# Lagged expert order, release-ordered weight units and three-pass output projections in a two-layer decoder kernel

## The chip, the cores and the metric

The kernel runs on one core of one Trainium2 chip. The metric is the device time of one execution in microseconds (us); lower is better. Engines are named as in the profile: PE is TensorE's matmul stream, PEld its loads of stationary operands, DVE is VectorE, ACT is ScalarE, POOL is GpSimd and SP is SyncE, which here only issues DMAs, in order.

## What is computed

A decoder trunk of two layers on 512 tokens of width 1024, in float32:

```python
for i in range(DEPTH):                      # DEPTH = 2
    if i % 2 == 0:                          # even: RWKV-7 heads beside sparse attention
        y = concatenate([rwkv7_time_mix(h), dsa_sparse_attention(h)])
        x = x + y @ ev_w_out                # 1024 x 1024
    else:                                   # odd: stick-breaking attention
        x = x + stick_breaking_attention(h) @ od_w_out
    x = x + hierarchical_moe(rmsnorm(x))    # top-1 of 4 groups, top-2 of 8 experts in it
return rmsnorm(x)
# an expert: (silu(xb @ w1) * (xb @ w3)) @ w2 ; w1, w3: 1024 x 512, w2: 512 x 1024 ; 32 experts a layer
```

All 32 experts' weights are read in each layer: 32 x 6 MB.

## The kernel before

A layer is a row of stages with a barrier between them: the mixer's stages (`even_mixer` or `odd_mixer`), `router`, `experts`. Tokens come in four tiles of 128.

**Weight units.** `ExpertWeights` (line 603) holds eleven units of 2 MB in SBUF. A piece is one matrix of one expert, numbered 3n + part (w1, w3, w2 of expert n), and piece p goes to unit p mod 11 (`place`, line 593). Units 8 and 9 (`GUEST`) hold the output projection's two halves until it is done; units 0 to 7 come free with the end of the mixer. SP loads pieces 0 to 7 at the start of `router` (line 358), piece 8 when all eight groups of the output projection are done, then waits for the scatter of the sorted rows, loads rows for three experts, and loads piece 9; piece 10 is the first of `experts` (line 863). From there `freed` (line 865) waits, piece by piece, for the unit's former user: `up_done` for w1 and w3, `down_done` for w2. The last two experts' w1 and w3 come in halves of 1 MB (`HALVED`). After the last piece SP loads, into units 8 and 9, what the next stage needs: three 1 MB chunks of the odd layer's projection in the first layer (`LoadedAhead`), the final gain in the second.

**Router.** For each tile i, PE does the output projection in two groups of 512 columns (h = 0, 1), each eight products of 128x128 by 128x512 in float32 (`out_project`, line 371). DVE adds each group to x (`add`, line 467); then PE transposes the tile (`turn`), DVE and ACT copy the transposed tile over the tile's place in `yT` (`empty_turned`, line 472, and line 445), and PE takes the router's logits from it (`logits`). PE's order is written out by hand: group (i+1, 0), turn(i), two of the eight steps of (i+1, 1), logits(i), the other six. DVE's first work in the stage is the scaling of the router's weights (line 513), which waits for their DMAs.

**Experts.** For each expert n, `up_expert` multiplies 48 rows by w1 and w3 (the two run beside each other in two column halves of the array, lines 723 and 724), `turn_hidden` transposes the hidden rows, `down_expert` multiplies by w2 (line 753), and `spread` (line 775) takes the result to the tokens by a selection matrix, in three-pass form; DVE adds it to x (line 820). `turn_rows` (line 711) transposes the next expert's rows. For n below `OWN` = 19 PE is lagged: up(n) is followed by turn_hidden(n-1) and down(n-1), with spread(n-2) in between. From `OWN` on each expert's up is followed by its own down, with spread(n-1). Between the two orders PE does down(18) before up(19) (lines 912 to 914).

**Three passes.** `three_passes` (line 1292) splits float32 operands into a rounded high part (fp32r, made by ACT) and a rest (fp32r, made by DVE) and multiplies high by high, high by low and low by high. The projections into q, k, v use it already.

**Chunks and attention of the even layer.** `rwkv_chunks` (line 2262) works on each tile by repeated squaring of small matrices, `squares(lv)` and `update(lv)`; `gram` (line 2395) makes products into two banks that DVE must have emptied. DVE fills gaps with `search.rounds` of the top-k search. `sparse_attend` (line 2669) goes through 16 units (4 tiles x 4 pairs of heads; 4 units for each length of 512, 384, 256, 128 keys): PE makes scores of two heads, DVE adds the mask (line 2752), DVE takes the negated maximum (line 2755), ACT takes the exponential and its sum (line 2792), DVE scales (line 2765), PE transposes, ACT copies, PE multiplies by the values.

## Time and profile before

| | |
|---|---|
| device time, three runs | 1745.83, 1750.96 (median), 1755.37 us |
| the profiled execution | 1747.62 us, span 1745.9 us |
| PE busy | 1632.2 us, 93% of the span |
| DVE, ACT, POOL busy | 56%, 26%, 9% |
| DMA moved | 475.40 MB, mean 272 GB/s |

PE is the clock of the whole kernel by its busy share, but the share is an average: in the two expert stages (about 478 to 950 us and 1261 to 1735 us) the DMA engines are also full. A row of the timeline gives the start, the duration, the engine, the line, the operation, the tiles and the count, then idle time in front in square brackets with its releaser. A float32 product is two PE instructions in the profile.

### The profile page before, as it was taken

The page shows a single profiled execution, that of the slowest core. Times are in us where ns is not written, and L with a number is a line of the kernel's source. Part 1 is how long each engine was busy: PE and PEld are TensorE (multiplying, and loading weights), DVE is VectorE, ACT ScalarE, POOL GpSimd, SP SyncE. Part 2 cuts the span into 40 slices and gives each one's busy share as a digit, 9 for nine tenths or more (in the row PEclk, how much of TensorE's full clock was granted, in tenths as well). Part 3 has the DMA queues.
Part 4 walks back from the last instruction along what each step waited for, and adds up shares of the span by engine and source line. Part 5 has one row for each costly group of instructions (what it writes and reads, how often), then busy time and mean ns, then how long its engine had stood idle before and what let it go on. Part 6 is the DMA issues. An engine that isn't in the chain of part 4 may idle for free. (4 is left out here: it accounts for less than half of the span.)

```text
span 1745.9 us, 27516 instructions
## 1 busy us (share of the span) xinstructions
PE 1632.2 (93%) x11158; PEld 875.4 (50%) x11287; DVE 977.9 (56%) x1657; ACT 459.5 (26%) x777; POOL 157.0 (9%) x188
## 2 busy tenths in 40 slices
PE   7999877889899999999998999999899999999996
PEld 6756666655533333333334977665533333333333
DVE  4548566581336666676666322561336666666666
ACT  4353444372311111111112321462211111111112
POOL 2002524310100000000000040120100000000000
PEclk9999999999999999999999999999999999999998
DMA  6441000028599999999996250208699999999993
GB/s 200 115 127 55 7 3 4 5 96 307 230 370 425 426 425 425 427 425 424 426 422 229 77 193 24 97 2 332 227 384 425 427 424 425 426 426 425 425 421 160
DMA packets 102256, 475.40 MB, mean 272 GB/s; under 512 B 28913, under 2 KB 67825, under 8 KB 76528
## 3 DMA queue, kind: packets, MB, share of 16 engines
q1 hardware_dynamic: 98752, 461.03, 65.5%
q0 software_dynamic: 3376, 12.58, 1.9%
q8 instruction: 91, 1.49, 0.4%
q14 instruction: 37, 0.30, 0.0%
HBM read 454.71 MB, written 18.87 MB: 271 GB/s over the span
## 5 line engine op out<-in xcount | busy, mean ns | idle before, releaser
L723 PE MATMUL ps<-w_unit,xT 128*48 128x512 f32 x1024 | 451.9, 594 | 3.8 <-DVE xT L780 3.0
L724 PE MATMUL ps<-w_unit,xT 128*48 128x512 f32 x1024 | 452.0, 594 | 0.0
L820 DVE SCALAR_TENSOR_TENSOR x<-ps,gate_by_expert,x 128x512 f32<-128x512 f32 x512 | 348.3, 744 | 178.2 <-PE ps L775 178.1
L723 PEld LDWEIGHTS ps<-w_unit,xT 128*48 128x48 f32 x1024 | 125.9, 123 | 308.9 <-issue 305.5
L753 PE MATMUL ps<-w_unit,hidT 128*48 128x512 f32 x1024 | 247.2, 603 | 12.1 <-issue 12.1
L775 PE MATMUL ps<-y_high_low,slots_to_tokens 128*128 128x512 f32 x512 | 154.3, 422 | 8.1 <-DVE y_high_low L795 5.2
L843 ACT ACTIVATE y_high_low<-ps 48x512 fp32r<-48x512 f32 x128 | 75.8, 592 | 322.1 <-PE ps L753 320.5
L775 PEld LDWEIGHTS ps<-y_high_low,slots_to_tokens 128*128 128x128 f32 x512 | 86.1, 188 | 123.2 <-DVE x L820 57.0
L1294 PE MATMUL ps<-hT_high,w_high 128*128 128x512 f32 (+1 forms) x336 | 135.5, 403 | 7.1 <-PE ps L1296 4.0
L836 ACT ACTIVATE gate_act_hid<-ps 48x512 f32<-48x512 f32 x64 | 37.9, 593 | 372.3 <-PE ps L724 372.3
L1296 PE MATMUL ps<-hT_high,w_low 128*128 128x512 f32 (+1 forms) x336 | 133.0, 396 | 0.0
L1295 PE MATMUL ps<-hT_low,w_high 128*128 128x512 f32 (+1 forms) x336 | 132.5, 394 | 0.0
L724 PEld LDWEIGHTS ps<-w_unit,xT 128*48 128x48 f32 x1024 | 125.9, 123 | 0.0
L753 PEld LDWEIGHTS ps<-w_unit,hidT 128*48 128x48 f32 x1024 | 60.0, 122 | 119.2 <-issue 119.2
L788 DVE TENSOR_TENSOR gate_act_hid<-gate_act_hid,ps 48x512 f32<-48x512 f32 x64 | 44.3, 692 | 127.9 <-ACT gate_act_hid L836 110.9
L377 PE MATMUL ps<-w_unit,yT 128*128 128x512 f32 x256 | 113.8, 596 | 1.7 <-PEq L78 1.7
L795 DVE TENSOR_TENSOR y_high_low<-ps,y_high_low 48x512 fp32r<-48x512 f32 x128 | 88.1, 688 | 25.7 <-ACT y_high_low L843 22.7
L1294 PEld LDWEIGHTS ps<-hT_high,w_high 128*128 128x128 f32 (+1 forms) x336 | 63.3, 188 | 33.1 <-issue 17.7
L377 PEld LDWEIGHTS ps<-w_unit,yT 128*128 128x128 f32 x256 | 47.3, 190 | 54.6 <-issue 54.6
L1296 PEld LDWEIGHTS ps<-hT_high,w_low 128*128 128x128 f32 (+1 forms) x336 | 63.2, 188 | 15.1
L1295 PEld LDWEIGHTS ps<-hT_low,w_high 128*128 128x128 f32 (+1 forms) x336 | 63.3, 188 | 14.5 <-issue 0.2
L1278 DVE TENSOR_TENSOR w_low<-w_unit,w_high 128x2048 fp32r<-128x2048 f32 (+1 forms) x13 | 28.6, 2196 | 60.3 <-ACT w_high L1264 60.2
(368 smaller groups left out, 1972.2 us busy)
## 6 DMA issues: line engine op xcount, KB each, us to landing
w_unit<-in_moe_w SPq DMA_DIRECT2D x184, 2048.0 KB, 28.3
w_unit<-in_moe_w SPq DMA_DIRECT2D x16, 1024.0 KB, 33.0
x_rows<-sorted_rows SPq DMA_DIRECT2D x64, 192.0 KB, 26.5
w_unit<-in_od_w_qkv SPq DMA_DIRECT2D x12, 1024.0 KB, 5.5
w_raw<-in_ev_w_in SPq DMA_DIRECT2D x10, 1024.0 KB, 6.1
sorted_rows<-bias SPq DMA_DIRECT2D x32, 192.0 KB, 5.6
w_unit<-in_ev_w_out SPq DMA_DIRECT2D x2, 2048.0 KB, 10.6
w_unit<-in_od_w_out SPq DMA_DIRECT2D x2, 2048.0 KB, 11.3
```

The lines of the kernel that those rows point to most:

```text
L377: last = nc.tensor.matmul(ps_out[2 * (i % 2) + h][:, :], yT[:, f, tok(i)], w[h][:, f, :], start=f == 0, stop=f == KD - 1)
L723: nc.tensor.matmul(ps_1[0:MB, :], xT[b][:, k, :], w1[:, k, :], start=k == 0, stop=k == KD - 1)
L724: last = nc.tensor.matmul(ps_3[UP:UP + MB, :], xT[b][:, k, :], w3[:, k, :], start=k == 0, stop=k == KD - 1)
L753: last = nc.tensor.matmul(ps_y[h][half[h], :], hidT[:, k, :], w2[:, k, h * FF:(h + 1) * FF], start=k == 0, stop=k == KF - 1)
L775: nc.tensor.matmul(ps_c[t % 2 * 2 + h][:, :], sel_of(n)[:, t * P:(t + 1) * P], y[:, h, :], start=True, stop=True).then_inc(spread_out, 1)
L788: nc.vector.tensor_tensor(hid, gate_act, ps_3[UP:UP + MB, :], ALU.mult).then_inc(hid_done, 1)
L795: nc.vector.tensor_tensor(y[half[1 - h], h, :], ps_y[h][half[h], :], y[half[h], h, :].bitcast(F32), ALU.subtract).then_inc(low_out, 1)
L820: nc.vector.scalar_tensor_tensor(out=xs, in0=ps_c[i % 4][:, :], scalar=gate(t), in1=xs, op0=ALU.mult, op1=ALU.add).then_inc(added, 1)
L843: nc.scalar.activation(y[half[h], h, :], ps_y[h][half[h], :], ACT.Copy).then_inc(high_out, 1)
L1294: nc.tensor.matmul(out, lhsT[0], rhs[0], start=start, stop=False)
L1295: nc.tensor.matmul(out, lhsT[0], rhs[1], start=False, stop=False)
L1296: return nc.tensor.matmul(out, lhsT[1], rhs[0], start=False, stop=stop)
```

## The change

- `OWN` becomes 31 from 19: all experts but the last are lagged.
- Units are given to pieces in the order in which the lagged order releases them (`in_order_of_release`, `places`), and `freed` waits accordingly.
- The first four pieces behind the eleven (3's w2 and 4's w1, w3, w2) come in halves of 1 MB, each issued when its unit's first or second half has been used (`load_early`).
- Expert 0 uses another PSUM bank, and the transposes of expert 1's rows move into the middle of up(0).
- Tiles 1 to 3 of the output projections go in three passes. Their high parts live in units 5, 6 and 7 (`LENT`), their low parts over the originals (`wl` is units 8 and 9, `yT_low` lies over `yT`). ACT makes the high parts: 8 weight pieces of 1024 columns and 3 tiles. DVE makes the low parts.
- So only pieces 0 to 4 are loaded at the start of `router`. Pieces 5 and 8 are issued at the seventh group, pieces 6, 7 and 9 behind the scatter and the rows.
- What is loaded ahead for the next stage waits for each guest unit's own last user.
- In `rwkv_chunks` the gram product of the second kind goes behind update(1), and two search rounds go in front of its reading on DVE.
- In `sparse_attend` the add and the maximum become one `tensor_tensor_reduce` for each head, and scores are kept negated.

```diff
--- before.py
+++ after.py
...
+    y_high, y_low, w_high, w_low = (c.sem(n) for n in ("y_high", "y_low", "w_out_high", "w_out_low"))
+    w_out, lent = wts.guest(), wts.lent()
+    wh, yT_high, wl = lent[0:2], lent[2], lent[3:5]
...
-            wts.load(sp, range(GUEST[0]))
-            sp.wait_ge(out_done, 2 * TT)
+            wts.load(sp, range(LENT[0]))
+            sp.wait_ge(out_done, 2 * TT - 1)
+            wts.load(sp, LENT[:1])
             wts.load(sp, GUEST[:1])
             for j in range(2):
                 sp.wait_ge(scattered[j], 16 * TT)
             for n in range(SLOTS):
                 r.load_rows(sp, xrows, n, n * CAP)
+            sp.wait_ge(out_done, 2 * TT)
+            wts.load(sp, LENT[1:])
             wts.load(sp, GUEST[1:])
...
-                    last = nc.tensor.matmul(ps_out[2 * (i % 2) + h][:, :], yT[:, f, tok(i)], w[h][:, f, :],
-                                            start=f == 0, stop=f == KD - 1)
+                    out = ps_out[2 * (i % 2) + h][:, :]
+                    if i == 0:
+                        last = nc.tensor.matmul(out, yT[:, f, tok(i)], w[h][:, f, :], start=f == 0, stop=f == KD - 1)
+                    else:
+                        if f == 0:
+                            pe.wait_ge(y_low, i)
+                        if i == 1 and f % 2 == 0:
+                            pe.wait_ge(w_low, h * HALF + f // 2 + 1)
+                        last = three_passes(nc, out, [part[:, f, tok(i)] for part in (yT_high, yT_low)],
+                                            [part[h][:, f, :] for part in (wh, wl)], f == 0, f == KD - 1)
...
+            def round_tile(i):
+                nc.scalar.activation(yT_high[:, :, tok(i)], yT[:, :, tok(i)], ACT.Copy).then_inc(y_high, 1)
+
+            round_tile(1)
+            for h in range(2):
+                act.wait_ge(wts.guest_in[h], 16)
+                for f in range(0, KD, 2):
+                    nc.scalar.activation(wh[h][:, f:f + 2, :], w_out[h][:, f:f + 2, :], ACT.Copy).then_inc(w_high, 1)
+                round_tile(2 + h)
...
+            def lower_tile(i):
+                dve.wait_ge(y_high, i)
+                V.tensor_tensor(yT_low[:, :, tok(i)], yT[:, :, tok(i)], yT_high[:, :, tok(i)].bitcast(F32),
+                                ALU.subtract).then_inc(y_low, 1)
+
+            def lower_weights(h, n):
+                dve.wait_ge(out_done, h + 1)
+                dve.wait_ge(w_high, h * HALF + n + 1)
+                fs = slice(2 * n, 2 * n + 2)
+                V.tensor_tensor(wl[h][:, fs, :], w_out[h][:, fs, :], wh[h][:, fs, :].bitcast(F32),
+                                ALU.subtract).then_inc(w_low, 1)
+
+            lower_tile(1)
+            lower_tile(2)
+            for n in range(HALF):
+                lower_weights(0, n)
             add(0, 0)
             add(0, 1)
+            lower_weights(1, 0)
+            lower_weights(1, 1)
             for i in range(LAST):
+                if i == 0:
+                    lower_weights(1, 2)
+                    lower_weights(1, 3)
+                    lower_tile(3)
                 add(i + 1, 0)
...
+LENT = (5, 6, 7)
...
+LAST, OWN = N_EXP - 1, N_EXP - 1
+
+
+def in_order_of_release():
+
+    pieces = [(0, 0), (0, 1)]
+    for n in range(1, OWN):
+        pieces += [(n, 0), (n, 1), (n - 1, 2)]
+    pieces += [(OWN - 1, 2)]
+    for n in range(OWN, N_EXP):
+        pieces += [(n, 0), (n, 1), (n, 2)]
+    return pieces
+
+
+def places():
+
+    released, where, uses = in_order_of_release(), {}, [0] * UNITS
+    for p in range(N_EXP * len(PARTS)):
+        j = p if p < UNITS else where[released[p - UNITS]][0]
+        where[divmod(p, len(PARTS))] = j, uses[j]
+        uses[j] += 1
+    return released, where, uses
+
+
+RELEASED, PLACES, LOADS = places()
...
+EARLY = [divmod(p, len(PARTS)) for p in range(UNITS, UNITS + 4)]
+IN_HALVES = EARLY + [(n, part) for n in HALVED for part in range(2)]
...
-    ps_x, ps_h, ps_y, ps_1, ps_3, ps_c = ps[0], ps[1], (ps[2], ps[2]), ps[3], ps[3], ps[4:8]
+    ps_x, ps_h, ps_y, ps_c = ps[0], ps[1], (ps[2], ps[2]), ps[4:8]
+    ps_up = lambda n: ps[4] if isinstance(n, int) and n == 0 else ps[3]
...
-    LAST, OWN = N_EXP - 1, 19
...
-        if not isinstance(n, int) or n >= 1:
+        if not isinstance(n, int) or n >= 2:
...
+            if isinstance(n, int) and n < len(EARLY) // 2 and k == KD // 2 - 1:
+                last.then_inc(up_half, 1)
...
+            if n == 0:
+                turn_rows(pe, 1, 0)
...
+        if isinstance(n, int) and n == 1:
+            act.wait_ge(hid_done, n)
...
+            def load_early(gone):
+                for half_, done in enumerate((up_half, up_done)):
+                    sp.wait_ge(done, gone + 1)
+                    for piece in EARLY[2 * gone:2 * gone + 2]:
+                        wts.load_half(sp, *piece, half_)
 
             for n in range(SLOTS, N_EXP):
                 sp.wait_ge(xT_done, n - SLOTS + 1)
                 r.load_rows(sp, xrows, slot(n), n * CAP)
-                if n in HALVED:
+                if n - SLOTS < 2:
+                    load_early(n - SLOTS)
+                elif n in HALVED:
...
-                sp.wait_ge(down_done, max(users) + 1)
-                ahead.load(sp, [wts.unit[j] for j in GUEST])
+                ahead.load(sp, [wts.unit[j] for j in GUEST], lambda i: sp.wait_ge(down_done, users[i] + 1))
...
             up_expert(pe, 0, -1)
-            turn_rows(pe, 1, 0)
...
                     squares(lv)
-                    if lv == 1:
-                        gram((B[2], B[3]), ka, both, False, 2 * CH)
                     if lv > 1:
                         update(lv - 1)
+                    if lv == 2:
+                        gram((B[2], B[3]), ka, both, False, 2 * CH)
...
+                before, between, behind, last = ROUNDS[t]
+                search.rounds(dve, min(2, before))
                 for par in range(2):
                     o = B[2 + par].read(dve)[:, :].rearrange("p (f m n) -> p f m n", f=FT, m=2)
                     B[2 + par].empty(V_.tensor_tensor(NQ[:, par, :, :, :], o, later, ALU.mult))
-                before, between, behind, last = ROUNDS[t]
-                search.rounds(dve, before)
+                search.rounds(dve, before - min(2, before))
...
-                        pe.wait_ge(biased, i - 1)
+                        pe.wait_ge(maxed, 2 * i - 2)
...
-                    bias = m.bias[:, t, 0:L].rearrange("p (o l) -> p o l", o=1).to_broadcast([P, 2, L])
-                    V_.tensor_tensor(lg[i % DEEP][:, :, 0:L], ps_z[i % 2][:, :, 0:L], bias,
-                                     ALU.add).then_inc(biased, 1)
-                    dve.wait_ge(biased, i + 1)
-                    V_.tensor_reduce(nmax[:, i, :], lg[i % DEEP][:, :, 0:L], AX.X, ALU.max,
-                                     negate=True).then_inc(maxed, 1)
+                    for a in range(2):
+                        V_.tensor_tensor_reduce(out=lg[i % DEEP][:, a, 0:L], in0=ps_z[i % 2][:, a, 0:L],
+                                                in1=m.bias[:, t, 0:L], scale=-1.0, scalar=-4.0 * NEG, op0=ALU.add,
+                                                op1=ALU.min, accum_out=nmax[:, i, a:a + 1]).then_inc(maxed, 1)
...
+                        act.wait_ge(maxed, 2 * i + a + 1)
                         nc.scalar.activation(lg[i % DEEP][:, a, 0:L], lg[i % DEEP][:, a, 0:L], ACT.Exp,
-                                             bias=nmax[:, i, a:a + 1], accum_out=tot[:, i, a:a + 1]).then_inc(exped, 1)
+                                             bias=nmax[:, i, a:a + 1], scale=-1.0, accum_out=tot[:, i, a:a + 1]).then_inc(exped, 1)
...
```

`up(1)` waits for no other expert's product any more, since expert 0 has its own bank; the view functions, `arrived` and the semaphores of the halves are changed to match.

## Rows read from the trace of the kernel before

**Rows 1.** The page: what the DMA engines moved in each fortieth of the span.
```profile
GB/s 200 115 127 55 7 3 4 5 96 307 230 370 425 426 425 425 427 425 424 426 422 229 77 193 24 97 2 332 227 384 425 427 424 425 426 426 425 425 421 160
```
**Rows 2.** Three stretches; last columns: TensorE clock, DMA share, GB/s.
```profile
490.00:500.00 10.00, 8.50 (x42) 3.00 (x41) 1.25 (x2) 0.59 (x1) 0.00 (x0) 1.00 0.93 366
500.00:510.00 10.00, 9.96 (x50) 3.91 (x50) 3.64 (x6) 2.11 (x4) 0.00 (x0) 1.00 0.69 273
...
1285.00:1290.00 5.00, 5.00 (x26) 1.76 (x24) 2.52 (x5) 1.18 (x2) 0.00 (x0) 1.00 0.42 128
```
**Rows 3.** PE's timeline: two row transposes; up(29), up(31) of either layer.
```profile
682.32 0.55 PE L711 MATMUL ps<-ident,x_rows 128*128 128x128 f32 x3
696.31 0.55 PE L711 MATMUL ps<-ident,x_rows 128*128 128x128 f32 x3
...
899.25 0.60 PE L723 MATMUL ps<-w_unit,xT 128*48 128x512 f32 x1 [0.78 <-DMA w_unit<-in_moe_w]
...
928.31 0.59 PE L723 MATMUL ps<-w_unit,xT 128*48 128x512 f32 x1
...
1681.66 0.59 PE L723 MATMUL ps<-w_unit,xT 128*48 128x512 f32 x1
...
1710.69 0.59 PE L723 MATMUL ps<-w_unit,xT 128*48 128x512 f32 x1
```
**Rows 4.** PE's timeline where the lagged order ends, layer one then two.
```profile
743.70 0.68 PE L745 MATMUL ps<-ident,gate_act_hid 48*128 48x48 f32 x4
...
751.38 1.92 PE L753 MATMUL ps<-w_unit,hidT 128*48 128x512 f32 x8
...
1525.76 0.68 PE L745 MATMUL ps<-ident,gate_act_hid 48*128 48x48 f32 x4
...
1530.14 3.26 PE L753 MATMUL ps<-w_unit,hidT 128*48 128x512 f32 x8
...
1536.49 0.59 PE L723 MATMUL ps<-w_unit,xT 128*48 128x512 f32 x1
```
**Rows 5.** SP's timeline: the first rows' loads in layer one and two.
```profile
478.45 1.28 SPq L1052 DMA_DIRECT2D x_rows<-sorted_rows  x3
...
1260.78 1.28 SPq L1052 DMA_DIRECT2D x_rows<-sorted_rows  x3
```
**Rows 6.** PE's timeline: output projection in either layer; first and last of 14 passes.
```profile
398.12 20.84 PE L377 MATMUL ps<-w_unit,yT 128*128 128x512 f32 x48 [0.92 <-PEq L78]
...
1180.54 20.84 PE L377 MATMUL ps<-w_unit,yT 128*128 128x512 f32 x48 [0.76 <-PEq L78]
...
1029.82 0.39 PE L1294 MATMUL ps<-hT_high,w_high 128*128 128x512 f32 x1
...
1032.84 0.39 PE L1295 MATMUL ps<-hT_low,w_high 128*128 128x512 f32 x1
```
**Rows 7.** DVE and ACT in the router's stage, and DVE's split of weights.
```profile
405.10 0.49 DVE L513 TENSOR_TENSOR w_router<-w_router,moe_gain 128x320 f32<-128x320 f32 x1 [10.92 <-DMA w_router<-in_moe_router_expert]
...
1189.45 0.49 DVE L513 TENSOR_TENSOR w_router<-w_router,moe_gain 128x320 f32<-128x320 f32 x1 [12.59 <-DMA w_router<-in_moe_router_expert]
...
952.90 1.23 DVE L1278 TENSOR_TENSOR w_low<-w_unit,w_high 128x1024 fp32r<-128x1024 f32 x1
...
412.85 1.06 ACT L442 ACTIVATE xn<-x 128x1024 f32<-128x1024 f32 x1 [16.45 <-DVE x L470]
```
**Rows 8.** Sparse attention by form; the page's row of line 820.
```profile
L2752 DVE TENSOR_TENSOR prob<-ps,bias 128x1024 f32<-128x1024 f32 x4 | 4.9, 1220 | 1.4 <-PE ps L2707 1.4
L2755 DVE TENSOR_REDUCE minus_max<-prob 128x2 f32<-128x1024 f32 x4 | 4.9, 1220 | 0.1
...
L2792 ACT ACTIVATION_READ_ACCUMULATOR prob<-prob,minus_max 128x1 f32 x32 | 6.0, 189 | 0.0
...
L820 DVE SCALAR_TENSOR_TENSOR x<-ps,gate_by_expert,x 128x512 f32<-128x512 f32 x512 | 348.3, 744 | 178.2 <-PE ps L775 178.1
```
**Rows 9.** Chunks of the even layer: PE at its gram product (four such waits).
```profile
286.93 1.10 PE L2402 MATMUL ps<-kk_r,k 64*64 64x128 f32 x32 [1.76 <-DVE QbT L2628]
```

More of the change, by code:

```diff
@@ L589, with rounded_over @@
 GUEST = (8, 9)
+LENT = (5, 6, 7)
 EXTRA = (0, 1, 2)
+LAST, OWN = N_EXP - 1, N_EXP - 1
[15 more added lines that the diff above has]
+RELEASED, PLACES, LOADS = places()
 def place(n, part):
-    use, j = divmod(len(PARTS) * n + part, UNITS)
-    return j, use
+    return PLACES[n, part]
 HALVED = (N_EXP - 2, N_EXP - 1)
-LOADS = [sum(place(n, part)[0] == j for n in range(N_EXP) for part in range(len(PARTS))) for j in range(UNITS)]
+EARLY = [divmod(p, len(PARTS)) for p in range(UNITS, UNITS + 4)]
+IN_HALVES = EARLY + [(n, part) for n in HALVED for part in range(2)]
+def rounded_over(c, name, shape, side):
+    with ExitStack() as once:
+        return c.sb(name, shape, F32R, ctx=once, side=side)
 class ExpertWeights:
@@ L638, in load_half @@
         eng.dma_start(self.view(n, part)[:, rows, :], expert(self.dram[part], n, 2 * k)[:, rows, :]).then_inc(
-            self.rest_landed[HALVED.index(n)][part] if half else self.landed[place(n, part)[0]], 16)
+            self.rest_landed[n, part] if half else self.landed[place(n, part)[0]], 16)
     def arrived(self, pe, n, part):
@@ L1537, in odd_mixer @@
     ctx = c.ctx.enter_context(ExitStack())
+    yT_low = rounded_over(c, "yT_low", [P, KD, T], "left")
     yT = c.sb("yT", [P, KD, T], ctx=ctx)
```

48 lines of the change are left out of this document (29 added, 19 removed).

## The prediction

> **What bounds the kernel now.** I read the slices of the DMA engines first. In both expert stages they move 422 to 427 GB/s in every slice but those at their ends [rows 1]; I take 425. An expert needs three pieces of 2048 KB and 192 KB of rows, 6.49 MB; at 425 GB/s that is 15.27 us. PE takes less: the lagged order has a period of 13.99 us, and two experts of the order without lag take 29.06, so 14.53 each [rows 3]. DMA is thus slower than PE by 1.28 us an expert, and what hides it is the lead of the eleven units. The lead is used up at the end: up(29) waits 0.78 us for its weights [rows 3]. So at up(29) of layer one both limits meet, and in layer two they nearly do. From there on the stage's end is set by what PE still has to do, two periods without lag up to up(31). What a faster PE saves before up(29) it will lose in waits; what counts is when the weights of expert 29 land, and the PE work behind it.
>
> **When the weights land.** DMA is continuous from the load of the rows (478.45 and 1260.78 [rows 5]) but for small holes. Holes from 490 to 510: 0.7 + 3.1 = 3.8 us; in layer two 0.58 x 5 = 2.9 us [rows 2]. They come from waits for units to be freed. A piece is 2.097 MB, 4.93 us. When the rows are issued, nine pieces are there now; after the change seven (0 to 5 and 8), since 6, 7 and 9 are issued behind the scatter. That costs 2 x 4.93 = 9.86 us of DMA per layer. The early halves close the holes: behind the rows the queue has pieces 6, 7, 9 and 10, 20 us of work, and up(0) frees half a unit before that. So the holes' 3.8 and 2.9 are gained in full; at worst none.
>
> **The router's length.** In float32 48 instructions, 24 products, take 20.84 us, 0.868 a product; 13 steps of one pass take 3.02 us, so three passes 0.697 [rows 6]. 48 products (tiles 1 to 3) at 0.171 save 8.2 us. By the Trainium skill (FP8 and Floating Point Precision, TensorE Precision Notes) true float32 is four passes; three would be 0.651 and save 10.4, and the sum would be some 4 us lower over both layers. The row has three passes at four fifths, and it decides.
>
> Against that stand the splits. ACT has 8 weight pieces and 3 tiles of 1024 columns at 1.06 each [rows 7], 11.7 us, inside tile 0's 13.9 us of float32 products. DVE is the tight one. It begins behind the scaled router weights, 405.6, 7.5 us after PE's first product, and 9.4 us after it in layer two [rows 6, 7]. Then, at 1.23 a split [rows 7] (about 1.2 apart): two tiles and four weight pieces, two adds of 0.69, four more pieces, tile 3, an add and the copy of tile 0's transposes. From 405.6 this is 11 x 1.2 + 3 x 0.65 + 0.65 = 15.8, so 421.4. PE, unheld, has done tile 1's first half at 412.0 + 5.6, turn(0) 0.9 and two steps 1.4: 419.9, and then the logits need that copy. PE stands 1.5 us in layer one and, DVE being 1.9 later, 3.4 in layer two. Net the router is shorter by 6.7 and 4.8. Bounds: 8.2 if DVE's splits are covered, 0 if they are half as long again. A stand at the logits holds nothing else up: positions and destinations come a tile later.
>
> So expert 29's weights land, in layer one, at 899.25 - 6.7 - 3.8 + 9.9 = 898.6. In layer two, where nothing shows the landing, I take the same distance from the rows' issue as in layer one, 420.8, less 0.9 for the smaller holes: 1680.7; up(29) began at 1681.66 [rows 3], which fits. It becomes 1680.7 - 4.8 - 2.9 + 9.9 = 1682.9. PE by itself could be there over 20 us earlier (shorter router, ten periods at 13.99 for 14.53, and the end of the lag, 9.5, not yet paid), so DMA sets this point.
>
> **The work behind it.** Lagged, up(29) is followed by two periods, 28.0 us. Then the lag ends: turn_hidden(30), a wait for DVE to split what down(29) has just left, spread(29), down(30), up(31). At 19 this took 743.70 to 753.2 (the last down at 751.38 and 1.85 of it), 9.5 us, and 1525.76 to 1536.49, 10.7 us, in layer two, where the down behind the wait ran 3.26 us in place of 1.92, as at a lower clock [rows 4]. So up(31) starts at 898.6 + 28.0 + 9.5 = 936.1 against 928.31, and at 1682.9 + 28.0 + 10.7 = 1721.6 against 1710.69 [rows 3]: **+7.8 and +10.9 us**. Before, the end of the lag was paid at expert 19, in front of DMA's limit, where the lead covered it; now it comes behind. Weights of 30 and 31 don't bind: 31's second halves are 30.5 us behind 29's, up(31) 37.5. From up(31) the order is the old one. The third chunk loaded ahead now waits for down(31), some 14 us after up(31), but is wanted third in the next stage; two are issued at down(29). I count nothing; if the next stage stood for it, 2 us.
>
> **The even layer's two stages.** In sparse attention DVE's add and maximum take 1.22 each for 512 keys and two heads [rows 8], 2.44 a unit. The fused form is two instructions; the nearest row in kind, one that combines a PSUM and an SBUF operand twice, takes 0.744 for 512 [rows 8]. With nothing for the accumulator it is 1.49; with ACT's accumulator read, 0.189 [rows 8], each, 1.87. So 0.6 to 0.95 saved a unit at 512 keys, and less at fewer, where fixed costs double: over 16 units 2.5 to 7.5 us of some 46, the lower end nearer since two short ops replace one. At half rate it would lose 2. I take -4. The Trainium skill (VectorE: DVE Perf Modes, Two Vector instructions with no wait between them) says an op that also writes its accumulator is two instructions, an argument against the fused form; ACT has such reads, 32 of them [rows 8], and no row of DVE shows one.
>
> In the chunks PE stands 1.76 us in front of the second gram product for DVE [rows 9], in each of four tiles. Moved behind update(1) it lets the squares go on, but then 1 us of gram lies in front of squares(3), which had been waiting for ACT anyhow, and DVE reads later. At most 7 us, at least 0 (DVE's two rounds could be late for the next user of the bank): I take -4.
>
> **The sum.** Against the profiled execution's 1747.62: +7.8 + 10.9 - 4 - 4 = +10.7, so **1758.3 us**. The runs' median, 1750.96, lies 3.3 above that execution, and the three runs spread over 9.5; that spread is why 0.5% (8.8 us) is about what can be told from no change here.
>
> **Rivals.**
> *The expert stages are PE's* (faster). If DMA had a reserve when PE asks sooner, so that an expert's 6.49 MB came within 13.99 us (464 GB/s; the point of decision), every saving of PE would stay: per layer the router's 6.7 or 4.8 and 12 x 0.54 = 6.5 of lag. That is -13.2, -11.3 and -8 for the even stages: 1715. For it: PE is busy 93% and shows one wait for weights in 64 experts. Against it: 425 GB/s in slice after slice, the same to 1%, however PE's period was at the time. 0.10.
> *The gains at their upper ends* (same). Attention 7, chunks 6, and the splits are covered: -5 and -5 more, 1749. For it: DVE is nearly full in attention. 0.23.
> *The three passes save nothing.* If DVE's splits or ACT's strided pieces take half as long again, PE stands the 6.7 and 4.8 that it was to save, and the weights start later by as much: 1758.3 + 11.5 = 1770. For it: layer two has a margin of less than nothing already. 0.12.
> *My forecast*, 1751 to 1765: 0.55; six parts in ten of it lie above 0.5%.
>
> **Chances.** Faster by over 0.5%: 0.10 and 0.03 of the second rival, 0.13. Slower: 0.33 and 0.12, 0.45. Within: 0.42. The range leaves out the first rival and half of the third: 1744 to 1770; forecast and second rival make it so wide.
>
> **What would show it.** PE waiting about 1.3 us for weights at most experts from about the thirteenth, up(29) near 899 and 1683 less 8 for the stages in front, and 37 to 39 us from it to up(31). DMA slices at 425. An issue of rows 5 to 7 us sooner after the router's start. PE standing 1 to 4 us before tile 0's logits. Wrong would be: no waits for weights, or up(29) more than 5 us sooner; a fused op of over 0.95 us at 512 keys; output projection steps above 0.75.

## The result and the profile after

The changed kernel takes 1772.49 us (median of four runs, 1768.29 to 1775.84) against 1753.16 (1745.83 to 1786.35) for the kernel before on the same chip: ratio 1.0138, interval 1.0116 to 1.016; the ratio is taken over fast executions alone, which leaves out 1786.35 (the other three have a median of 1750.96, which alone gives 1.0123). It is slower, by more than I forecast: 1758.3 us, range 1744 to 1770. That is 21 to 24 us where I had forecast 10.7. The profiled execution is the longest of its four, 1775.84 us; that is 28.2 above the profiled execution of before, of which about 6 seem to be that execution's own and not the change's, as the parts below show.

The page of the kernel after. Its weights' line, 811, was line 723 before:

```profile
GB/s 197 113 124 54 7 3 4 59 42 262 285 423 424 426 426 425 426 424 426 425 419 91 96 184 6 96 4 262 267 422 425 425 425 426 426 425 425 426 419 74
...
L811 PE MATMUL ps<-w_unit,xT 128*48 128x512 f32 x1024 | 454.1, 596 | 35.6 <-DMA w_unit<-in_moe_w 35.6
```

DMA moves 422 to 426 GB/s in the full slices of the stages (419 in the last of them), as in [rows 1]. New is the last column of line 811: PE idles 35.6 us ahead of its up products for weights, where the timeline of before shows a single wait of 0.78 us in both expert stages [rows 3].

PE's timeline after, the same instructions as in [rows 3]: up(15) and up(16), up(29) and up(31) of layer one, then of layer two.

```profile
682.81 0.60 PE L811 MATMUL ps<-w_unit,xT 128*48 128x512 f32 x1 [0.84 <-DMA w_unit<-in_moe_w]
698.06 0.60 PE L811 MATMUL ps<-w_unit,xT 128*48 128x512 f32 x1 [1.05 <-DMA w_unit<-in_moe_w]
...
898.74 0.60 PE L811 MATMUL ps<-w_unit,xT 128*48 128x512 f32 x1 [0.98 <-DMA w_unit<-in_moe_w]
...
938.84 0.59 PE L811 MATMUL ps<-w_unit,xT 128*48 128x512 f32 x1
...
1700.03 0.60 PE L811 MATMUL ps<-w_unit,xT 128*48 128x512 f32 x1 [0.98 <-DMA w_unit<-in_moe_w]
...
1738.90 0.59 PE L811 MATMUL ps<-w_unit,xT 128*48 128x512 f32 x1
```

698.06 - 682.81 = 15.25: from up(15), the first that waits, every expert takes DMA's time and not PE's 13.99 us. Most periods up to up(29) are 15.2, a few 15.6 to 16.2, and the mean is 15.42. Before, up(31) came 29.06 us behind up(29); now it comes 40.10 and 38.87 behind it. Between these two nothing waits for weights. What lies there is the end of the lag, at expert 31 in place of 19 (compare [rows 4]). PE's timeline after, in layer one:

```profile
926.96 0.68 PE L837 MATMUL ps<-ident,gate_act_hid 48*128 48x48 f32 x4
930.24 2.04 PE L867 MATMUL ps<-y_high_low,slots_to_tokens 128*128 128x512 f32 x4 [2.61 <-DVE y_high_low L887]
932.22 3.66 PE L845 MATMUL ps<-w_unit,hidT 128*48 128x512 f32 x8
...
937.08 1.92 PE L845 MATMUL ps<-w_unit,hidT 128*48 128x512 f32 x8
```

DVE's low part of expert 29 holds PE 2.61 us, and the down product behind it takes 3.66 us for 1.92: stretches after have PE's granted clock at 0.50 there (columns as in [rows 2]):

```profile
932.00:936.00 4.00, 4.00 (x10) 0.86 (x10) 1.92 (x3) 0.00 (x0) 0.00 (x0) 0.50 0.95 304
```

**The books.** SP issues the first rows at 473.51 and 1273.58:

```profile
473.51 1.29 SPq L1152 DMA_DIRECT2D x_rows<-sorted_rows  x3
...
1273.58 1.28 SPq L1152 DMA_DIRECT2D x_rows<-sorted_rows  x3
```

PE's first product of the output projection is at 394.37 (398.12 in [rows 6]). I take as a router stage's start SP's first issue in it, 0.05 us earlier in layer one of either kernel, 1180.49 and 1192.73 in layer two.

| stretch | before | after | predicted change | measured change |
|---|---|---|---|---|
| start to router 1 | 398.06 | 394.32 | -8 | -3.7 |
| router 1 to rows | 80.39 | 79.19 | -6.7 | -1.2 |
| rows to up(29) | 420.80 | 425.23 | +6.1 | +4.4 |
| up(29) to up(31) | 29.06 | 40.10 | +8.4 | +11.0 |
| up(31) to router 2 | 252.18 | 253.89 | 0 | +1.7 |
| router 2 to rows | 80.29 | 80.85 | -4.8 | +0.6 |
| rows to up(29) | 420.88 | 426.45 | +6.0 | +5.6 |
| up(29) to up(31) | 29.03 | 38.87 | +9.7 | +9.8 |

The two lines of the router are what I had wrong: 10.9 us of savings that did not come. The first line is partly this execution's own (eleven of the twelve runs below have the even layer's new stages, and their first router stage starts between 386.0 and 393.1, in the middle at 390.3), and so is the fifth (252.2 or 253.9 in one run or another, with either kernel's loads ahead). Against the forecast these two lines make 6.0 us. From the first masked scores of the sparse attention (350.10 and 349.44) to the router's start it is 47.96 us before and 44.88 after; the other 0.7 us of the first line's 3.7 come from the stages ahead of attention, where b_even, below, gains 4.5 and a_whole 8.9. So it is there that this execution was slow; no other execution of the kernel after has a trace.

**The router.** The three passes do what they should. PE's timeline in tile 1's first group and at tile 0's logits, then DVE's splits up to there:

```profile
410.96 0.40 PE L1397 MATMUL ps<-w_rounded,w_rounded 128*128 128x512 f32 x1
...
411.66 0.40 PE L1397 MATMUL ps<-w_rounded,w_rounded 128*128 128x512 f32 x1
...
416.66 1.95 PE L411 MATMUL ps<-w_router,yT 128*128 128x40 f32 x16 [0.46 <-DVE yT L498]
```

```profile
401.55 2.35 DVE L539 TENSOR_TENSOR yT_low<-yT,w_rounded 128x1024 fp32r<-128x1024 f32 x2
403.82 4.62 DVE L546 TENSOR_TENSOR w_rounded<-w_unit,w_rounded 128x1024 fp32r<-128x1024 f32 x4
...
414.10 1.22 DVE L539 TENSOR_TENSOR yT_low<-yT,w_rounded 128x1024 fp32r<-128x1024 f32 x1
```

411.66 - 410.96 = 0.70 a product, as worked out, and the eleven splits hold PE 0.46 us at tile 0's logits (0.70 in layer two), where I had 1.5 and 3.4. What takes the saving away stands some 40 us later, where I had not looked. ACT's and PE's timelines after, at tile 3:

```profile
459.55 1.06 ACT L465 ACTIVATE xn<-x 128x1024 f32<-128x1024 f32 x1 [12.02 <-DMA sorted_rows<-xn,dest]
...
460.61 0.58 ACT L468 ACTIVATE yT<-ps 128x512 f32<-128x512 f32 x1
```

```profile
454.07 1.06 PE L411 MATMUL ps<-w_router,yT 128*128 128x40 f32 x8 [0.43 <-DVE yT L498]
461.24 1.93 PE L411 MATMUL ps<-w_router,yT 128*128 128x40 f32 x8 [6.11 <-ACT yT L468]
```

For the normalization ACT squares each tile and throws the squares into `xn[i % 2]`, the buffer from which the scatter of tile i-2 reads. Tile 3's squares therefore wait for tile 1's scatter, and ACT's half of the copy of the transposed tile 3, which PE's last logits need, stands behind the squares in ACT's queue. ACT waits 12.02 us, PE 6.11 (13.51 and 7.59 in layer two). Before there was such a wait too, a tile earlier, and it cost nothing. ACT's and PE's timelines before:

```profile
449.44 1.06 ACT L442 ACTIVATE xn<-x 128x1024 f32<-128x1024 f32 x1 [9.55 <-DMA sorted_rows<-xn,dest]
...
463.18 1.06 ACT L442 ACTIVATE xn<-x 128x1024 f32<-128x1024 f32 x1 [6.22 <-DVE x L470]
```

```profile
464.79 1.95 PE L397 MATMUL ps<-w_router,yT 128*128 128x40 f32 x16 [0.43 <-DVE yT L475]
```

Behind the stand PE's clock is lower, though a_late, below, shows that this is not the stand's doing alone. Stretches after (columns as in [rows 2]):

```profile
445.00:455.00 10.00, 9.37 (x60) 8.16 (x58) 3.89 (x17) 2.30 (x2) 3.03 (x4) 1.00 0.95 389
455.00:460.00 5.00, 0.12 (x2) 0.01 (x1) 0.00 (x0) 0.45 (x1) 0.81 (x1) 0.83 0.97 359
460.00:465.00 5.00, 3.76 (x24) 3.76 (x25) 1.72 (x11) 4.75 (x6) 0.00 (x0) 0.50 0.19 76
...
490.00:500.00 10.00, 9.96 (x49) 3.68 (x49) 2.26 (x4) 1.07 (x3) 0.00 (x0) 1.00 1.00 424
500.00:510.00 10.00, 10.00 (x49) 4.26 (x49) 4.20 (x7) 1.96 (x4) 0.00 (x0) 1.00 1.01 416
```

After PE stood from 455 to 460 its granted clock is 0.50 from 460 to 465, the lower of its two levels. From 445 to 460 the DMA engines are full: SP issues units 5 and 8, 4.2 MB, at the seventh group (443.5 to 444.3), and POOL issues tile 1's scatter at 445.35, right behind. The last rows show the holes of [rows 2] closed, as predicted.

### The profile page after: what moved, and what is told of

It is laid out like the page before. It is cut to its first block and busy times, and to the rows that moved or that the text cites. A ratio compares the mean times of both kernels' runs of the same rounds, so it can differ in the third digit from the quotient of the medians.

```text
span 1774.0 us, 27826 instructions
## 1 busy us (share of the span) xinstructions
PE 1635.0 (92%) x11254; PEld 911.5 (51%) x11383; DVE 990.1 (56%) x1711; ACT 480.6 (27%) x799; POOL 155.5 (9%) x188
## 5 line engine op out<-in xcount | busy, mean ns | idle before, releaser
L811 PE MATMUL ps<-w_unit,xT 128*48 128x512 f32 x1024 | 454.1, 596 | 35.6 <-DMA w_unit<-in_moe_w 35.6
L811 PEld LDWEIGHTS ps<-w_unit,xT 128*48 128x48 f32 x1024 | 123.9, 124 | 338.5 <-issue 338.3
L812 PEld LDWEIGHTS ps<-w_unit,xT 128*48 128x48 f32 x1024 | 123.9, 124 | 0.0
L112 PE MATMUL ps<-half 128*128 128x128 bf16 x772 | 57.6, 236 | 7.0 <-PEq L78 6.8
L1634 DVE TENSOR_TENSOR_SCAN tail<-keep,zero 128x512 f32<-128x512 f32 (+3 forms) x64 | 49.4, 814 | 23.1 <-POOL keep L1621 23.1
L880 DVE TENSOR_TENSOR gate_act_hid<-gate_act_hid,ps 48x512 f32<-48x512 f32 x64 | 44.2, 691 | 30.0 <-ACT gate_act_hid L930 15.6
## 6 DMA issues: line engine op xcount, KB each, us to landing
w_unit<-in_ev_w_out SPq DMA_DIRECT2D x2, 2048.0 KB, 10.7
```

The costliest lines, as they stand in the source:

```text
L112: nc.tensor.matmul(ps[:, 0:P], c.half[:, :], c.half[:, :], start=True, stop=True)
L811: nc.tensor.matmul(ps_up(n)[0:MB, :], xT[b][:, k, :], w1[:, k, :], start=k == 0, stop=k == KD - 1)
L812: last = nc.tensor.matmul(ps_up(n)[UP:UP + MB, :], xT[b][:, k, :], w3[:, k, :], start=k == 0, stop=k == KD - 1)
L1634: nc.vector.tensor_tensor_scan(tail[i % DEEP][:, a, 0:L][:, ::-1], keep[i % DEEP][:, a, 0:L][:, ::-1], zero[:, 0:L], 1.0, ALU.mult, ALU.ad ...
```

## The experiments

Two theories. **A**: in each expert stage the end of the lag, about 10 us of PE's time, was hidden at expert 19 because PE led there, and is paid in full behind the point that DMA sets. **D**: the scatter that ACT's squares wait for stands behind the loads of the lent units, and this costs the router what three passes save. Rivals of A: the weights' order and the later loads cost it; rival of D: DVE's splits, or the scatter by itself. In the table d is the distance from the rows' issue to up(29), layer one / layer two; before has 420.8 / 420.9. The last three columns are from one profiled execution of each. The runs were made on several chips, each beside the kernel before on the same chip (medians 1745.9 to 1748.6 us), so runs are compared by their ratios.

| run | median us | ratio [interval] | router to rows | d | up(29) to up(31) |
|---|---|---|---|---|---|
| a_own19 | 1753.78 | 1.0035 [1.0016, 1.0053] | 79.3 / 80.4 | 427.2 / 427.9 | 29.1 / 29.0 |
| b_own31 | 1764.42 | 1.0089 [1.0066, 1.0113] | 80.5 / 80.3 | 420.0 / 419.6 | 38.9 / 40.3 |
| a_late | 1760.46 | 1.0068 [1.0047, 1.0090] | 72.6 / 73.7 | 425.5 / 426.1 | 38.9 / 39.0 |
| a_no3p | 1751.51 | 1.0019 [1.0003, 1.0035] | 81.2 / 80.3 | 416.5 / 415.6 | 39.4 / 39.0 |
| a_hold | 1773.47 | 1.0153 [1.0133, 1.0174] | 70.8 / 73.0 | 435.6 / 436.0 | 38.7 / 37.6 |
| b_even | 1739.92 | 0.9960 [0.9945, 0.9976] | 80.5 / 79.8 | 421.3 / 419.0 | 29.0 / 29.0 |
| a_no3p_own19 | 1737.19 | 0.9937 [0.9922, 0.9951] | 80.6 / 80.1 | 419.4 / 419.5 | 29.0 / 29.0 |
| a_own19_late | 1739.44 | 0.9959 [0.9944, 0.9973] | 72.5 / 73.6 | 426.3 / 426.8 | 29.0 / 29.0 |
| a_no3p_own25 | 1743.70 | 0.9974 [0.9960, 0.9988] | 80.2 / 80.2 | 423.5 / 423.5 | 29.0 / 29.0 |
| a_own25 | 1761.55 | 1.0077 [1.0061, 1.0094] | 79.3 / 80.0 | 433.8 / 433.7 | 29.0 / 29.0 |
| a_whole | 1770.44 | 1.0127 [1.0111, 1.0143] | 79.1 / 80.3 | 426.0 / 425.9 | 39.0 / 38.9 |
| a_own13_late | 1736.18 | 0.9934 [0.9911, 0.9956] | 72.5 / 73.9 | 425.2 / 426.4 | 29.1 / 29.0 |

**The end of the lag, undone and done alone.** In the kernel after, back to 19:

```diff
-LAST, OWN = N_EXP - 1, N_EXP - 1
+LAST, OWN = N_EXP - 1, 19
```

> The changed kernel with OWN back at 19, so that the lag ends at expert 19 again; units still go by the order of release. Theory A (the end of the lag costs when it lies behind the point where DMA sets the pace): up(29) stays where it is in either layer, up(31) comes 29 us behind it instead of 38.9 to 40.1, so about 20 us are saved over both layers and the kernel stands 2 to 8 us above the one before. Rival B (the slower time comes from the router and the later loads alone, the place of the lag's end is indifferent): no change to within 5 us of the changed kernel's +24. Rival C (the lag hides PE work that shows again without it): up(29) comes later by up to 6 us a layer and the saving is under 10 us in all.

It gave back 1.38% - 0.35% = about 1.0%, 18 us. In the kernel before, `OWN` from 19 to 31 and nothing else:

```diff
-    LAST, OWN = N_EXP - 1, 19
+    LAST, OWN = N_EXP - 1, N_EXP - 1
```

> The kernel before with OWN = 31 and nothing else, units in their old order. Theory A: up(29) still lands with DMA, at its old distance of 420 to 421 us from the rows' issue, PE waits for weights at most experts from the thirteenth or so, up(31) is 38 to 39 us behind up(29), and the kernel is 19 to 22 us slower than before. Rival B: within 5 us of the kernel before, since PE saves 6.5 us a layer and pays the end once as ever.

It lost 0.9%, 16 us. The point up(29) moves by at most 2.0 us against the rows in either run, while the piece behind it changes by 9.8 to 11.3: theory A, from both sides. I had expected 19 to 22 us of b_own31; its profiled execution, the longest of its four, is 21 above that of before, its median 16. The waits begin at up(19), not at the thirteenth. In b_own31 PE's timeline of layer one has up(29) where it was, waiting for weights a little longer than in [rows 3], and only then turn_hidden(30), with which the lag's end begins:

```profile
898.77 0.60 PE L723 MATMUL ps<-w_unit,xT 128*48 128x512 f32 x1 [0.97 <-DMA w_unit<-in_moe_w]
...
926.99 0.68 PE L745 MATMUL ps<-ident,gate_act_hid 48*128 48x48 f32 x4
```

**The squares freed of the scatter.** The squares go into a scratch tile, and ACT waits for the scatter only ahead of the scaled rows, which do need `xn`:

```diff
-                if i >= 2:
-                    act.wait_ge(scattered[i % 2], 32 * (i // 2))
-                nc.scalar.activation(xn[:, i % 2, :], x[:, t, :], ACT.Square,
+                nc.scalar.activation(squared[:, :], x[:, t, :], ACT.Square,
...
+                if i >= 2:
+                    act.wait_ge(scattered[i % 2], 32 * (i // 2))
                 nc.scalar.activation(xn[:, i % 2, :].rearrange(
```

> The changed kernel, but the squares of a tile are written to a bf16 scratch tile, and ACT waits for the scatter of two tiles ago only in front of the scaled rows. Theory D (in the router PE stands 6.1 us because ACT's squares wait for the scatter of tile 1, and that scatter lies behind the two units issued at the seventh group): PE's wait at tile 3's logits goes, the clock does not fall there, the rows' issue comes 5 to 8 us sooner after the router's start in either layer, and the kernel gains 10 to 15 us. Rival E (the scatter itself ends as late as before, so only the place of the wait changes): the rows' issue moves by less than 2 us, the kernel by less than 3.

The router stage is 72.6 and 73.7 us long, 6.6 and 7.1 less than after, and 7.8 and 6.6 less than before; the runs gain 0.7%, 12 us. ACT's timeline of a_late (tile 3's squares; the scaled rows have the wait now):

```profile
447.39 1.06 ACT L464 ACTIVATE squared<-x 128x1024 bf16<-128x1024 f32 x1 [4.92 <-DVE x L494]
...
454.74 2.18 ACT L475 ACTIVATE xn<-x,rstd 128x1024 f32<-128x1024 f32 x1 [5.36 <-DMA sorted_rows<-xn,dest]
```

One thing came otherwise than expected: the clock still falls. Without the stand, PE's granted clock is 0.66 from 450 to 455 (0.50 from 452 to 454), with PE busy all of that time and 4.4 of the 5 us before. So the low clock of the kernel after can't be put down to its stand alone.

**Is the scatter late because of the loads?** The kernel after, with units 5 and 8 issued with 6, 7 and 9 behind the scatters:

```diff
-            sp.wait_ge(out_done, 2 * TT - 1)
-            wts.load(sp, LENT[:1])
-            wts.load(sp, GUEST[:1])
...
-            wts.load(sp, LENT[1:])
-            wts.load(sp, GUEST[1:])
+            wts.load(sp, LENT)
+            wts.load(sp, GUEST)
```

> The changed kernel with the loads of the two units that it issues at the seventh group held back behind the scatters with the others; nothing else is changed. If the scatter was late because it stood behind these 4.2 MB, as theory D says, ScalarE's wait for the scatter ahead of tile 3's squares shrinks from 12.0 us to under 6, TensorE's 6.1 us ahead of the last logits go, router to rows is 72 to 74 us, and the DMA point comes 5 to 10 us later from the rows (430 to 435): 1765 to 1780 us, ratio about 1.01. Rival (the scatter itself takes that long): the wait stays at 9 to 12 us and router to rows at 79.

ACT's squares of tile 3 wait for DVE's sum alone (4.93 us), as in a_late, though the wait for the scatter still stands ahead of them, and the last logits start 0.43 us behind their copy:

```profile
448.70 1.06 ACT L462 ACTIVATE xn<-x 128x1024 f32<-128x1024 f32 x1 [4.93 <-DVE x L490]
```

```profile
450.32 1.95 PE L408 MATMUL ps<-w_router,yT 128*128 128x40 f32 x16 [0.43 <-DVE yT L495]
```

So it was the loads. The clock is 1.00 from 440 to 460 in layer one, but 0.50 from 1250 to 1255 in layer two, again without a stand. The router is 8.4 and 7.8 us shorter than after, and up(29) comes 10.4 and 9.6 later from the rows, which is the 9.86 us of two units (I had expected 430 to 435 for d, it is 435.6 and 436.0): as a whole the run is as slow as the kernel after. The two ways to load these units cost about the same.

**The router stage of before in the kernel after** (f32 output projections, eight units loaded ahead, one unit at the eighth group). It leaves out no part of the computation. Its core:

```diff
-            wts.load(sp, range(LENT[0]))
-            sp.wait_ge(out_done, 2 * TT - 1)
-            wts.load(sp, LENT[:1])
+            wts.load(sp, range(GUEST[0]))
+            sp.wait_ge(out_done, 2 * TT)
```

> The changed kernel with the router's stage as before: all tiles in float32, pieces 0 to 7 loaded at its start, 8 at the eighth group, 9 behind the scatter. Order of units, lag, early halves and the even layer's stages stay as changed. By theory A and the ledger: the router's length is as before (80.3 us to the rows' issue), up(29) comes 3 to 4 us sooner than before in distance from the rows' issue (417, the holes closed), up(31) 38 to 40 us behind it. So 20 us for the end of the lag, less 7 for the holes, less 3 to 4 for the even layer: 8 to 12 us above the kernel before. If the lent units were harmless instead, it would stand at the changed kernel's +24 or above, since the three passes' gain is gone.

It is 1.2% faster than the kernel after: the three passes, as they stand in the change, cost some 20 us. Against before it is 0.19% slower, 3 us, where I had expected 8 to 12. I had put the even layer's part at 3 to 4 us, which b_even shows to be 7, and the closed holes at 7, which are 9.6 here. The router is 2.0 us longer without them in layer one and 0.5 shorter in layer two, and d is shorter by 8.7 and 10.9 (425.2 to 416.5, 426.5 to 415.6). That is the two units, 9.86.

**The even layer's parts alone**, in the kernel before (gram product behind update(1), fused add and maximum). Its core:

```diff
-                    if lv == 1:
-                        gram((B[2], B[3]), ka, both, False, 2 * CH)
...
+                    if lv == 2:
+                        gram((B[2], B[3]), ka, both, False, 2 * CH)
...
-                    V_.tensor_reduce(nmax[:, i, :], lg[i % DEEP][:, :, 0:L], AX.X, ALU.max,
-                                     negate=True).then_inc(maxed, 1)
+                    for a in range(2):
+                        V_.tensor_tensor_reduce(out=lg[i % DEEP][:, a, 0:L], in0=ps_z[i % 2][:, a, 0:L],
```

> The kernel before with only the even layer's move of the gram and rounds and the fused multiply with reduce. Both theories: the first router stage starts at about 390 us (398.1 before), everything behind it is as before: 8 us, 1740 to 1742 us, ratio 0.9955. Rival (the 8 us are given back later, by loads that the expert stage then waits for): under 3 us, ratio 0.998 to 1.000.

1739.92 us, 0.9960: the first router stage starts at 390.45, 7.6 us sooner, and nothing is given back. Of the 7.6, 3.1 lie between the first masked scores (350.10 before, 345.57 here) and the router, 4.5 ahead of them. In the view of PE's waits from 275 to 345 us the kernel before has the first row, and b_even (seen from 270 on) none of the kind; its longest class with a named releaser is the second:

```profile
PE ps L2402 <- DVE QbT L2628: 3.5, 2, 1.8
```

```profile
PE ps L2524 <- DVE minusU L2654: 2.2, 3, 1.2
```

**Repairs together.** The kernel after with the router of before and the end of the lag at 19, and the kernel after with the free squares and the end at 19. In both, besides the diff of a_no3p or of a_late:

```diff
-LAST, OWN = N_EXP - 1, N_EXP - 1
+LAST, OWN = N_EXP - 1, 19
```

> The changed kernel with the router stage of before (f32 output projections, eight units loaded ahead) and with the end of the lag at its old place (19). Theory A (the lag's end behind the point that the DMA sets costs about 10 us a layer) and theory D (the router loses what three passes gain to the wait for a scatter that stands behind the lent units' loads) together: router to rows 80 to 81 us as before, the point up(29) 417 to 420 us behind the rows, up(31) 29.1 behind it, with the even layer's and chunks' 8 us kept: 1736 to 1742 us, ratio 0.993 to 0.996 against before. Rival (what a_no3p leaves is made of something else, weights' order or the return in two steps): 1748 or more, ratio 1.00.

> The changed kernel with the end of the lag at 19 and with the squares freed of the scatter's wait. Theories A and D together: router to rows 72 to 73 us, up(29) 427 to 428 us behind the rows (the DMA sets it, its last loads ask no sooner for that), up(31) 29.1 behind it: 1740 to 1745 us, ratio 0.994 to 0.997. Rival (the two repairs overlap, because what the router gives back the DMA takes at up(29)): 1752 to 1755, ratio 1.002 as with the lag's end alone.

Both ratios came as expected: 0.9937 and 0.9959. The first has no wait for weights at all; in it up(29) is PE's own. Side by side they also say that the three passes gain nothing as a whole even when the squares are free: the router is 8.1 and 6.6 us shorter with them, d is 7.0 and 7.2 longer, and the intervals of the two ratios overlap. The interval of the first overlaps that of b_even alone (0.9960) too, so the order of release and the early halves have no gain of their own that is clear of noise.

**The end of the lag in between.** `OWN = 25`, with the router of before and with that of the change:

```diff
-LAST, OWN = N_EXP - 1, N_EXP - 1
+LAST, OWN = N_EXP - 1, 25
```

> The changed kernel with the router stage of before and the end of the lag at 25, to see whether the point at which the DMA sets up(29) is where theory A puts it (416 us behind the rows with eight units loaded ahead, as the run with the end of the lag at 31 showed). Theory A: six more periods at 13.99 in place of 14.53 bring TensorE to up(29) 3.2 us sooner, 419.4 to 416.2, just at the DMA's point; up(31) still 29.0 behind: 3 us a layer less than with 19, 1730 to 1733 us, ratio 0.990 to 0.992. Rival (the end of the lag costs the same wherever it stands): up(31) comes as late as with the end at 31, 1750.

> The changed kernel, the end of the lag at 25 and nothing else. Theory A: the DMA sets up(29) at 425 to 427 us behind the rows, as with the end at 19 and at 31, and up(31) comes 29.1 behind it: the same time as with 19, 1752 to 1756 us, ratio 1.002 to 1.005; the waits for weights sum to 8 to 12 us a layer. Rival (TensorE sets the point): 3 us a layer less than with 19, ratio 1.000 or less.

Both expectations failed: by their ratios they were slower than with 19, by 0.37% and 0.42%, 6.5 and 7.3 us. I had taken the DMA's point as something that only up(29) meets. PE's timeline of a_no3p_own25, layer one (the rows are up(23), up(24), spread(23) and up(25)):

```profile
796.83 0.60 PE L777 MATMUL ps<-w_unit,xT 128*48 128x512 f32 x1 [1.51 <-DMA w_unit<-in_moe_w]
812.07 0.60 PE L777 MATMUL ps<-w_unit,xT 128*48 128x512 f32 x1 [1.03 <-DMA w_unit<-in_moe_w]
829.62 2.04 PE L833 MATMUL ps<-y_high_low,slots_to_tokens 128*128 128x512 f32 x4 [2.64 <-DVE y_high_low L853]
...
838.23 0.59 PE L777 MATMUL ps<-w_unit,xT 128*48 128x512 f32 x1
```

PE meets DMA at up(21) already, and from there every expert is DMA's. The end of the lag then makes a period of 26.16 us (838.23 - 812.07): up(25) starts 365.5 us behind the rows, against 354.7 in a_no3p, which has its lag's end at 31. PE is 10.8 late. From there to up(29) it takes four periods of 14.50, 58.0 us, while DMA takes 61.9 in a_no3p (three of 15.2 and one of 16.2). That regains 3.9, and 7.0 remain: d is 423.5 against 416.5. So the end of the lag costs 10.9 us, less PE's lead where it stands, less about 0.75 for each expert from there to up(29). Some 15 experts are wanted. That makes a test, a_own19_late with the end at 13:

```diff
-LAST, OWN = N_EXP - 1, 19
+LAST, OWN = N_EXP - 1, 13
```

> The run with the squares freed of the scatter, the end of the lag at 13 in place of 19. Theory A as the run with the end at 25 corrected it (the end of the lag costs about 10.9 us, of which TensorE wins back 0.75 on each expert behind it, 15.25 of the DMA less 14.5 of the order without lag, so it is hidden only if 14 or more experts come behind it): up(12) at 166.4 behind the rows, up(13) at 191.3, TensorE alone would be at up(29) at 423.3, so the DMA sets it again, at 425.3 to 425.7; waits for weights only from up(27) on; up(31) 29.0 behind. That is 0.6 to 1.0 us a layer less than with 19 (426.3 and 426.8): 1737 to 1739 us, ratio 0.994 to 0.996. Rival (with the end at 19 the time was TensorE's, through and through): 3 us a layer more than with 19, up(29) at 429.

Measured: up(13) at 191.5 from the rows in layer one, first wait for weights at up(28) (at up(27) in layer two), up(29) at 425.2 and 426.4, 1736.18 us, 0.9934. PE's timeline shows up(29) DMA's again:

```profile
888.90 0.60 PE L812 MATMUL ps<-w_unit,xT 128*48 128x512 f32 x1 [0.47 <-DMA w_unit<-in_moe_w]
```

Against the end at 19 up(29) comes 1.1 and 0.4 us sooner; the two ratios, 0.9934 and 0.9959, have overlapping intervals, so by the whole time the test is not decided. This and a_no3p_own19 are the fastest of the runs; between these two the intervals don't decide either.

**The early halves.** The kernel after with the four pieces loaded whole:

```diff
-EARLY = [divmod(p, len(PARTS)) for p in range(UNITS, UNITS + 4)]
+EARLY = []
...
-                if n - SLOTS < 2:
-                    load_early(n - SLOTS)
-                elif n in HALVED:
+                if n in HALVED:
```

> The changed kernel with the four first pieces behind the eleven loaded whole (no early halves), in the order of release, the end of the lag at 31. If the early halves close the holes behind the rows, as my prediction's step had it: DMA slices under 0.9 appear between 490 and 515 us, and up(29) comes 3 to 4 us later from the rows than the 425.2 and 426.5 of the changed kernel: 1778 to 1781 us, ratio 1.019. Rival (with 20 us of loads queued behind the rows no hole would open anyhow): up(29) within 1 us, the same time as the changed kernel.

The rival was right. Stretches of a_whole, which issued its rows at 465.15:

```profile
480.00:490.00 10.00, 9.96 (x51) 3.65 (x51) 2.95 (x5) 1.25 (x3) 0.00 (x0) 1.00 1.01 429
490.00:500.00 10.00, 10.00 (x49) 3.98 (x47) 2.67 (x4) 1.78 (x3) 0.00 (x0) 1.00 1.01 426
```

There is no hole without them. What closed the holes is that two units more are still to be loaded behind the rows. Where eight units are loaded ahead, the change of orders, halves and expert 0's bank does close them: a_no3p against b_own31, both with the end at 31, has d shorter by 3.5 and 4.0, and moves 418 to 424 GB/s from 480 to 510. How much of that is the halves' and how much the other two's was not tried.

## Why the prediction was right and wrong

- **DMA sets up(29), 425 GB/s and 15.27 us an expert**: right (15.42 on average). The rival in which the expert stages are PE's is out: DMA gave no more when PE asked sooner.
- **Weights later by two units, +9.86 a layer**: right; a_no3p takes 8.7 and 10.9 back, a_hold's two units more cost 10.4 and 9.6.
- **Holes closed, -3.8 and -2.9**: right in size, d +4.4 and +5.6 for +6.1 and +6.0. The cause was wrong for this kernel: it was the longer queue, not the halves. So these were not two terms: of the 9.86 that the lent units cost, a part fills time in which the queue had idled: 3.8 and 2.9 by the holes, 5.4 and 4.3 by d.
- **The end of the lag behind up(29), 9.5 and 10.7**: right, if 2.6 us short in layer one. Measured 40.1 - 28.0 = 12.1 in layer one and 10.9 in layer two; the runs with the end at 31 have from 9.6 to 12.3, mostly 10.9. It was the largest term and the one that made the sign. What the step left out is that the end need not lie behind up(29) to cost: inside DMA's stretch it costs its 10.9 less 0.75 for each expert that follows up to up(29). Against the end at 31 and the same router stage, d is 7.0 to 8.6 longer at 25 and 0.7 to 3.9 at 19.
- **Attention and chunks, -4 and -4**: right in their sum; b_even gained 0.40%, 7 us, by its trace 3.1 in attention and 4.5 ahead of it. The fused form is the two instructions that I weighed, by form 687 ns for 512 keys plus 83 ns for reading the accumulator, 0.77 together where I had 0.93 at most. The Trainium skill (VectorE: DVE Perf Modes, Two Vector instructions with no wait between them) says that an op which also writes out its accumulator is two instructions, the main one and an accumulator read. The trace agrees: the read is a row of its own, of 83 ns. In the kernel after DVE's two rows are:

```profile
L2857 DVE CUSTOM_DVE_ANT_0 prob<-ps,bias 128x512 f32<-128x512 f32 x8 | 5.1, 687 | 1.2 <-PE ps L2812 1.2
...
L2857 DVE DVE_READ_ACCUMULATOR2_ANT minus_max<- 128x1 f32 x32 | 2.7, 83 | 0.0
```

- **The router, -6.7 and -4.8**: wrong, measured -1.2 and +0.6, and this is the step that failed. Its arithmetic held better than I thought: without the wait for the scatter, a_late has -7.8 and -6.6, since DVE began its splits 7.2 and 7.5 us behind the stage's start, where I had 7.5 and 9.4, at 1.16 each (four in 4.62). The step failed in its net sum, "Net the router is shorter by 6.7 and 4.8", and in the bounds under it, which set nothing but DVE's splits against the 8.2 us that three passes save. The wait for a scatter ahead of the last tile's logits was a term at nothing, without a reason. It measured 6.1 and 7.6 us of PE. The sentence that a stand at the logits "holds nothing else up" looks no further than tile 0. I followed the moved loads only as bytes that come later in the expert stage. I did not follow them to the DMA engines, which now have 4.2 MB to move when the scatter is issued, nor ask what ACT has queued behind the wait for that scatter. The rival "three passes save nothing" had nearly the right number, 1770, by luck: its reason, that the splits take half as long again, did not occur, and it had 0.12.

With -1.2 and +0.6 in the place of the two router terms my sum is 1758.3 + 10.9 = 1769.2. Of the 6.6 us left up to 1775.8, 6.0 are those of the stages ahead of the two routers, which the traces of the other runs mostly do not show. By the medians and the ratio the change costs 21.5 to 24 us against the forecast 10.7; the router's 10.9 are most or all of what was missing, and up to 2.5 stay open.

## What to carry to other kernels

When DMA is the slower of two full pipes, a fixed cost of the compute engine is free only where that engine leads, or where enough work stands behind it to catch up by the small difference of the two periods; find the first wait for data, and put such costs ahead of it or far enough from the end. Buffers lent to a neighbouring stage are paid for in DMA time at the far end, less only what the queue idled before. When a load is issued earlier, look which small transfer now stands behind it, and what sits in program order behind the wait for that transfer: a throwaway output in a buffer that a transfer still reads is enough to hold a whole engine.

## What was unexpected of the hardware

A tile's scatter (two indirect transfers of 128 rows of 4 KB), issued by POOL right behind 4.2 MB of SP's loads, took 12.4 and 12.6 us from issue to landing by the DMA view of the stretches around the two issues; the squares that wait for it run at 459.55. In a_hold, with the loads held back, the same two took 3.3 and 3.4 us, and the squares run at 448.70 with no wait for them.

```profile
446.61 0.96 POOL L623 DMA_INDIRECT sorted_rows<-xn,dest  x1 [0.30 <-issue]
```

```profile
442.86 0.96 POOL L620 DMA_INDIRECT sorted_rows<-xn,dest  x1 [0.30 <-issue]
```

The first row is from the kernel after's timeline of POOL, the second from a_hold's. The DMA view of the same stretch of the stage (440 to 475, and 435 to 470 in a_hold) gives the median from issue to landing of the six transfers of tiles 1 to 3, in the kernel after and then in a_hold:

```profile
sorted_rows<-xn,dest POOLq DMA_INDIRECT x6, 7.1
```

```profile
sorted_rows<-xn,dest POOLq DMA_INDIRECT x6, 3.5
```

That another engine issues a transfer did not spare it the loads in front. From 445 to 459.5 the engines moved about 5.5 MB (389 GB/s for 10 us, 359 for the rest), most of the 6.3 that had been issued: two units of 2.1 MB and two tiles' scatters of 1.05 MB. The Trainium skill (DMA: Bandwidth & Descriptors, Queues, rings and completion order) says that each DMA engine takes turns between the queues it has work for, packet by packet. If the turns were equal in bytes, an estimate from the rates above has tile 1's 1.05 MB done after some 2.1 MB of traffic, about 5 us; the trace has over 12, so either the turns were not equal in bytes or the scatter's packets came late. No run here tells which.

Behind a stand of 6.1 us TensorE's granted clock was 0.50 from 460 to 465, and with one of 2.61 us it was 0.50 from 930 to 936. But it was 0.50 from 452 to 454 in a_late and from 1250 to 1255 in a_hold too, where no such stand lies in front. What decides it these runs do not show.
